# Wide and narrow products of an expert chunk: interleaved, or eight and then eight

## The chip, the cores and the metric

One core of a Trainium2 chip runs the whole program in one launch. The time is device microseconds of that core; the figure to compare is the median of the runs. An engine here is TensorE (PE, matrix products; PEld is its weight load), VectorE (DVE), ScalarE (ACT), GpSimd (POOL) or SyncE (SP, which only issues transfers).

## What is computed

Two transformer blocks over 256 tokens of width 1024. Only the last part of the second block matters here, a PEER layer. Its experts are 16,384 rows of two tables, and a token uses 128 of them (8 heads of 16), with softmax weights g:

```python
u = jnp.take(u_tab, experts, axis=0)
v = jnp.take(v_tab, experts, axis=0)
act = jax.nn.gelu(jnp.einsum('td,thkd->thk', xb, u)) * g
return jnp.einsum('thk,thkd->td', act, v)
```

The kernel doesn't gather. It multiplies all tokens by the whole table u, in 128 chunks of 128 experts, takes the gelu, multiplies by a dense matrix of weights that is zero for experts not picked, and multiplies the result by the whole table v.

## The kernel before

**Products in three terms.** Every operand is held as the sum of two fp32r parts, a leading part and a rest. For a slab of weights (128 x 1024, a ring of three buffers `ring`, filled by SyncE), ScalarE copies the leading part into `wsplit[:, n, 0]` (`lead_scalar`, line 267), and VectorE or GpSimd subtracts it from the slab to give the low part `wsplit[:, n, 1]` (`rest_of`, line 273). `wsplit` has three buffers as well. GpSimd does the subtractions of chunks 0 to 117, VectorE those of the last ten. `hsplit` holds both parts of the tokens.

**One chunk.** `split_project_wide` makes a chunk: for each of eight 128-row pieces c, a 512-column product of the leading weights with both parts of the tokens (line 2735), and a 256-column product of the low weights with the tokens' leading part (line 2739), added to the upper 256 columns of the same PSUM bank. Both halves of the bank are added later. Chunks use banks 3, 4 and 5 in turn, and a chunk waits until the one three before it has been joined. The function first waits for the low part (`slab_split`), which comes after the leading one.

**ring_used.** Each slab raises this semaphore once, by its first product. `lead_scalar` for slab s waits until slab s - 2 has raised it: then slab s - 3, the last user of its `wsplit` buffer, is finished. So the lead copy of chunk c + 3 waits for the signal of chunk c + 1. SyncE refills a ring buffer when its subtraction is done.

**Early chunks, 0 to 53.** TensorE does chunk after chunk. ScalarE's order for chunk c: copy the upper half of the bank (the low copy, line 2763), lead copy of chunk c + 3, gelu of chunk c - 1 (line 2770). VectorE works through the top-16 picks of the layer and in between joins the halves of chunk after chunk (`joined_vector`, line 2782). At the end TensorE transposes the picks and VectorE sets up operands (lines 2870 to 2874).

**Spread batches, chunks 54 to 117.** There are 64 batches b, with chunk c = 54 + b. TensorE: chunk c, then eight small products (line 2923) of one-hot operands for four tokens, which wait for both operands of batch b (`hot` of 2b + 2), then the next chunk. ScalarE in its written order, with the waits that matter:

```python
low_scalar(act, c)                     # line 2950, waits for chunk c
lead_scalar(act, *chunk_of(c + 3))     # line 267, waits for ring_used
...                                    # weights of batch b, line 2964
gelu_scalar(act, c)                    # lines 2943, 2944
```

VectorE for batch b: first operand of batch b + 1 (`found_vector`, line 2979), join of chunk c (line 2955), second operand of batch b + 1 (`hot_vector`, line 2985), then a multiply over all chunks so far (line 3008, waits for line 2964), then the weighted product of chunk c (`late_vector`, line 2992, waits for the gelu). In the last two batches a subtraction (line 273) stands between line 2979 and line 2955.

**Last chunks, 118 to 127**: chunk after chunk again, with subtractions on VectorE. After them TensorE opens the outputs and the value slabs begin (line 424), twelve 512-column products each.

Of the kernel before, what the change touches and what calls it, by code (L numbers as in the profile page):

```python
# [31 lines left out]
P = 128  # L32
D = 1024
KC = D // P
T = 256
# [4 lines left out]
RING = 3  # L40
# [86 lines left out]
def build(nc, weights, small, tables, masks, w3, decay, subkeys, gain_row, x, out):  # L127
# [3 lines left out]
    def S(stage, what):  # L131

        name = f"{stage}_{what}"
        if name not in sems:
            sems[name] = ctx.enter_context(nc.semaphore(name))
        return sems[name]

    def sb(name, shape, dt=F32):
        return ctx.enter_context(nc.sbuf_tensor(name, shape, dt))

    ring = sb("ring", [P, RING, D])
    wsplit = sb("wsplit", [P, RING, 2, D], F32R)
    hsplit = sb("hsplit", [P, 2, KC, T], F32R)
# [18 lines left out]
    ps = ctx.enter_context(nc.psum_tensor("ps", [P, 8, 512], F32))  # L162
# [95 lines left out]
    def split_index(stream, k):  # L258
        return SPLIT[stream] + k
# [16 lines left out]
    def slab_split(pe, stream, k, i, per=6):  # L276

        which, before = RESTS[stream]
        pe.wait_ge(S("split", which), i * per + (before + k + 1))
        return split_index(stream, k) % RING  # L280
# [2448 lines left out]

    def split_project_wide(pe, bank, stream, k, i=0, per=6):  # L2730

        n = slab_split(pe, stream, k, i, per)
        both = ps[:, bank, :].rearrange("p (b t) -> p b t", b=2)
        for c in range(KC):
            mm = pe.matmul(both, wsplit[:, n, 0, c * P:(c + 1) * P], hsplit[:, :, c, :],  # L2735
                           start=(c == 0), stop=(c == KC - 1), skip_group_check=True)
            if c == 0:
                mm.then_inc(ring_used, 1)
            mm = pe.matmul(ps[:, bank, T:2 * T], wsplit[:, n, 1, c * P:(c + 1) * P], hsplit[:, 0, c, :],  # L2739
                           start=False, stop=(c == KC - 1), skip_group_check=True)  # L2740
        return mm

    def early_tensor(pe, st, stream):
        pe.wait_ge(S("final", "x_rows"), 2)
        for k in range(3):
            wide_tensor(pe, st, stream, k)
        with pe.Fori(0, EARLY // 6 - 1) as i:
            for k in range(3, 9):
                pe.wait_ge(S(st, "joined"), i * 6 + (k - 2))
                split_project_wide(pe, hidden_bank(k), stream, 16 + k, i).then_inc(S(st, "hidden"), 1)  # L2750
        for c in range(EARLY - 3, EARLY):
            wide_tensor(pe, st, stream, c)

    def wide_tensor(pe, st, stream, c):
        if c >= 3:
            pe.wait_ge(S(st, "joined"), c - 2)
        s, k = chunk_of(c)
        split_project_wide(pe, hidden_bank(c), s, k).then_inc(S(st, "hidden"), 1)
# [714 lines left out]
```

## Time and profile before

| | |
|---|---|
| Median of 3 runs | 1884.05 us (1883.6 to 1887.24) |
| Profiled execution, its time | 1885.56 us |
| Its span, first to last instruction | 1883.7 us |
| TensorE, VectorE, ScalarE, GpSimd busy | 98%, 74%, 55%, 18% |
| Granted TensorE clock, mean | 0.998 |
| Expert chunks, first to last product | 1128.7 to 1528.3 us of the span |

Times in rows are us from the start of the span, unless marked ns. "x16" is a number of instructions. What stands in brackets behind an instruction is how long its engine was idle before it, and what ended that. The products overlap each other: the distance from start to start is what one costs, and not its length.

### The profile page before, as it was taken

How to read it: one execution, taken by the hardware profiler on the slowest of the kernel's cores; microseconds unless marked ns; L12 is line 12 of the kernel's file. 1: busy time of each engine (PE TensorE's matmuls, PEld its weight loads, DVE VectorE, ACT ScalarE, POOL GpSimd, SP SyncE). 2: the span in 40 equal slices, each digit the busy share in tenths (PEclk: the TensorE clock that was granted, in tenths of full speed). 3: DMA queues.
4: the chain of work that ended last, by engine and by line, in shares of the span. 5: the costliest groups of instructions: out<-in, count | busy, mean ns of one | idle time of the engine just before them, and what ended most of it. 6: DMA issues, size and time to landing. Idle time of an engine off the chain costs nothing.

```text
span 1883.7 us, 32317 instructions
## 1 busy us (share of the span) xinstructions
PE 1853.5 (98%) x11238; PEld 1602.5 (85%) x11238; DVE 1401.9 (74%) x2658; ACT 1042.4 (55%) x1817; POOL 331.4 (18%) x145
## 2 busy tenths in 40 slices
PE   9999999999999999999999999999999999999998
PEld 7877887788888889999999998888888888888887
DVE  7785566667655568898997678977999976666666
ACT  6666455656644466667555555565665543333333
POOL 0000000000000000000000168886777400000000
PEclk9999999999999999999999999999999999999999
DMA  6624655443455544443445445554444455555554
GB/s 217 224 78 148 216 174 178 145 146 124 146 189 189 187 147 157 147 135 124 136 145 175 155 143 181 186 189 152 162 157 161 155 187 192 196 191 191 196 193 156
DMA packets 86157, 314.11 MB, mean 167 GB/s; under 512 B 9568, under 2 KB 9696, under 8 KB 85856
## 3 DMA queue, kind: packets, MB, share of 16 engines
q1 hardware_dynamic: 86048, 312.65, 49.2%
q8 instruction: 69, 1.13, 0.2%
q14 instruction: 40, 0.33, 0.1%
HBM read 311.56 MB, written 1.05 MB: 166 GB/s over the span
## 4 chain that ended last, share of the span: by engine, by line
PE 83%; DVE 13%; ACT 2%; issue 2%; DMA 0%; SPq 0%; DVEq 0%; ACTq 0%
PE ps L424 24%; PE ps L409 14%; PE ps L2735 11%; PE ps L290 6%; PE ps L1967 6%; PE ps L2739 6%; PE ps L2537 3%; DVE wsplit L273 3%; PE ps L819 2%; PE ps L2036 2%; PE ps L2923 1%; DVE sq L2979 1%; PE ps L440 1%; ACT wsplit L267 1%; DVE work L2300 1%
## 5 line engine op out<-in xcount | busy, mean ns | idle before, releaser
L267 ACT ACTIVATE wsplit<-ring 128x1024 fp32r<-128x1024 f32 x572 | 603.8, 1059 | 450.5 <-PE ps L424 265.4
L273 DVE TENSOR_TENSOR wsplit<-ring,wsplit 128x1024 fp32r<-128x1024 f32 x440 | 541.5, 1235 | 304.8 <-ACT wsplit L267 303.8
L424 PE MATMUL ps<-wsplit,gsplit 128*128 128x512 f32 x1992 | 456.5, 390 | 0.0
L424 PEld LDWEIGHTS ps<-wsplit,gsplit 128*128 128x128 f32 x1992 | 373.2, 188 | 81.3 <-issue 4.0
L273 POOL TENSOR_TENSOR wsplit<-ring,wsplit 128x1024 fp32r<-128x1024 f32 x132 | 317.2, 2404 | 664.5 <-ACT wsplit L267 664.2
L2735 PE MATMUL ps<-hsplit,wsplit 128*128 128x512 f32 x1024 | 368.6, 403 | 0.0
L409 PE MATMUL ps<-wsplit,hsplit 128*128 128x512 f32 x1248 | 298.1, 394 | 4.5 <-DVE wsplit L273 3.4
L2739 PE MATMUL ps<-hsplit,wsplit 128*128 128x256 f32 x1024 | 286.4, 280 | 0.0
L409 PEld LDWEIGHTS ps<-wsplit,hsplit 128*128 128x128 f32 x1248 | 231.6, 188 | 55.5 <-DVE wsplit L273 7.3
L290 PE MATMUL ps<-hsplit,wsplit 128*128 128x256 f32 x1956 | 253.6, 287 | 2.6 <-DVE hsplit L340 1.5
L290 PEld LDWEIGHTS ps<-hsplit,wsplit 128*128 128x128 f32 x1956 | 239.8, 191 | 10.4 <-issue 4.5
L2735 PEld LDWEIGHTS ps<-hsplit,wsplit 128*128 128x128 f32 x1024 | 193.1, 189 | 43.9 <-issue 0.4
L2739 PEld LDWEIGHTS ps<-hsplit,wsplit 128*128 128x128 f32 x1024 | 193.9, 189 | 0.0
L1967 PE MATMUL ps<-hsplit,wsplit 128*128 128x256 f32 x936 | 128.2, 288 | 0.0
L1967 PEld LDWEIGHTS ps<-hsplit,wsplit 128*128 128x128 f32 x936 | 115.9, 190 | 0.0
L792 POOL TENSOR_TENSOR sq<-sq 128x512 f32<-128x512 f32 x9 | 14.0, 1558 | 495.3 <-ACT sq L773 494.5
L2979 DVE TENSOR_TENSOR sq<-ps,picks 128x1024 f16<-128x1024 f32 x64 | 77.6, 1212 | 0.0
L2985 DVE TENSOR_TENSOR sq<-sq,ps 128x1024 f16<-128x1024 f16 x64 | 77.3, 1208 | 0.0
L2537 PE MATMUL ps<-hsplit,wsplit 128*128 128x256 f32 x576 | 71.1, 284 | 1.3 <-DVE hsplit L2518 0.9
L2537 PEld LDWEIGHTS ps<-hsplit,wsplit 128*128 128x128 f32 x576 | 69.6, 192 | 2.3 <-DVE wsplit L273 1.5
L2950 ACT ACTIVATE eyeiota<-ps 128x256 f32<-128x256 f32 x74 | 28.4, 384 | 67.1 <-PE ps L2739 66.2
L2078 ACT ACTIVATE work<-work 128x256 f32<-128x256 f32 x128 | 48.6, 430 | 23.0 <-DVE work L2220 17.0
(346 smaller groups left out, 1900.3 us busy)
## 6 DMA issues: line engine op xcount, KB each, us to landing
ring<-in_weights SPq DMA_DIRECT2D x572, 512.0 KB, 3.3
work<-in_weights SPq DMA_DIRECT2D x8, 512.0 KB, 5.8
work<-in_tables SPq DMA_DIRECT2D x1, 1995.0 KB, 9.8
work<-in_decay SPq DMA_DIRECT2D x2, 512.0 KB, 5.0
work<-in_subkeys SPq DMA_DIRECT2D x2, 512.0 KB, 4.4
out_x<-work SPq DMA_DIRECT2D x4, 256.0 KB, 2.4
gains_x<-in_x SPq DMA_DIRECT2D x3, 256.0 KB, 6.1
work<-in_small SPq DMA_DIRECT2D x1, 591.0 KB, 8.1
```

The lines of the kernel that those rows point to most:

```text
L267: act.activation(wsplit[:, n % RING, 0, :], slab(s), ACT.Copy).then_inc(S("split", "lead"), 1)
L273: eng.tensor_tensor(wsplit[:, n % RING, 1, :], slab(s), wsplit[:, n % RING, 0, :], ALU.subtract).then_inc(S("split", RESTS[stream][0]), 1)
L290: mm = pe.matmul(dst, wsplit[:, n, a, c * P:(c + 1) * P], h[:, b, :], start=(c == 0 and t == 0), stop=(c == KC - 1 and t == 2))
L409: mm = pe.matmul(ps[:, bank + tt, :], hsplit[:, b, c, tt * P:(tt + 1) * P], wsplit[:, n, a, cc * 512:(cc + 1) * 512], start=(c == 0 and t ...
L424: mm = pe.matmul(YR[:, tt, half * 512:(half + 1) * 512], gsplit[:, slot, b, tt * P:(tt + 1) * P], wsplit[:, n, a, half * 512:(half + 1) * ...
L1967: mm = pe.matmul(dst, wsplit[:, n, a, c * P:(c + 1) * P], hsplit[:, b, c, :], start=(c == 0 and t == 0), stop=(c == KC - 1 and t == 2))
L2078: ins = act.activation(strided(mixed, (l % 2 * 2 + x_) * T, [[2 * size, n], [size, 2], [1, size]]), strided(qakb, x_ * 2 * T, [[2 * size, ...
L2537: mm = pe.matmul(branch(m), wsplit[:, n, a, c * P:(c + 1) * P], hsplit[:, b, c, :], start=(c == 0 and t == 0), stop=(c == KC - 1 and t == 2))
L2735: mm = pe.matmul(both, wsplit[:, n, 0, c * P:(c + 1) * P], hsplit[:, :, c, :], start=(c == 0), stop=(c == KC - 1), skip_group_check=True)
L2739: mm = pe.matmul(ps[:, bank, T:2 * T], wsplit[:, n, 1, c * P:(c + 1) * P], hsplit[:, 0, c, :], start=False, stop=(c == KC - 1), skip_group ...
L2979: v.tensor_tensor(hots[:, b % 2, 0:2, :, :], strided(ps, 2 * 512, [[0, 2], [0, 4], [1, P]]), picks[:, 0:2, batch(b)].unsqueeze(3).to_broad ...
L2985: v.tensor_tensor(hots[:, b % 2, 2:4, :, :], hots[:, b % 2, 0:1, :, :].to_broadcast([P, 2, 4, P]), strided(ps, 2 * 512 + P + 4 * b, [[T if ...
```

## The change

The chunk waits for the leading weights alone, does its eight 512-column products, waits for the low part, and does its eight 256-column ones. The signal `ring_used` moves from the first wide product to the first narrow one. The products, their operands and the number of semaphore signals stay. All 128 chunks use this function; the value slabs and all other stages don't.

```diff
-        n = slab_split(pe, stream, k, i, per)
+        pe.wait_ge(S("split", "lead"), i * per + (split_index(stream, k) + 1))
+        n = split_index(stream, k) % RING
         both = ps[:, bank, :].rearrange("p (b t) -> p b t", b=2)
         for c in range(KC):
-            mm = pe.matmul(both, wsplit[:, n, 0, c * P:(c + 1) * P], hsplit[:, :, c, :],
-                           start=(c == 0), stop=(c == KC - 1), skip_group_check=True)
+            pe.matmul(both, wsplit[:, n, 0, c * P:(c + 1) * P], hsplit[:, :, c, :],
+                      start=(c == 0), stop=(c == KC - 1), skip_group_check=True)
+        slab_split(pe, stream, k, i, per)
+        for c in range(KC):
+            mm = pe.matmul(ps[:, bank, T:2 * T], wsplit[:, n, 1, c * P:(c + 1) * P], hsplit[:, 0, c, :],
+                           start=False, stop=(c == KC - 1), skip_group_check=True)
             if c == 0:
                 mm.then_inc(ring_used, 1)
-            mm = pe.matmul(ps[:, bank, T:2 * T], wsplit[:, n, 1, c * P:(c + 1) * P], hsplit[:, 0, c, :],
-                           start=False, stop=(c == KC - 1), skip_group_check=True)
         return mm
```

## Rows read from the trace of the kernel before

**Rows 1.** The page, busy time, share and instructions of each engine.

```profile
PE 1853.5 (98%) x11238; PEld 1602.5 (85%) x11238; DVE 1401.9 (74%) x2658; ACT 1042.4 (55%) x1817; POOL 331.4 (18%) x145
```

**Rows 2.** The page, chain that ended last, shares by line.

```profile
PE ps L424 24%; PE ps L409 14%; PE ps L2735 11%; PE ps L290 6%; PE ps L1967 6%; PE ps L2739 6%; PE ps L2537 3%; DVE wsplit L273 3%; PE ps L819 2%; PE ps L2036 2%; PE ps L2923 1%; DVE sq L2979 1%; PE ps L440 1%; ACT wsplit L267 1%; DVE work L2300 1%
```

**Rows 3.** Stretches that begin and end with a chunk: busy us, clock, DMA.

```profile
1128.73:1281.46 152.73, 152.73 (x868) 132.53 (x866) 123.59 (x328) 93.27 (x164) 128.81 (x55) 1.00 0.55 183
1287.76:1292.54 4.78, 4.78 (x28) 4.06 (x25) 3.59 (x6) 1.93 (x5) 2.39 (x1) 0.66 0.24 93
1292.54:1470.38 177.84, 177.84 (x1300) 152.91 (x1298) 173.43 (x270) 107.55 (x271) 128.85 (x54) 1.00 0.48 159
1470.38:1498.89 28.51, 27.41 (x197) 22.75 (x194) 28.51 (x42) 16.06 (x41) 15.17 (x7) 1.00 0.42 142
```

**Rows 4.** Timeline of an early chunk, which starts at 1137.30.

```profile
1137.30 0.40 PE L2735 MATMUL ps<-hsplit,wsplit 128*128 128x512 f32 x1
...
1137.53 0.28 PE L2739 MATMUL ps<-hsplit,wsplit 128*128 128x256 f32 x1
...
1139.05 2.41 POOL L273 TENSOR_TENSOR wsplit<-ring,wsplit 128x1024 fp32r<-128x1024 f32 x1 [0.55 <-ACT wsplit L267]
...
1140.32 0.39 ACT L2763 ACTIVATE work<-ps 128x256 f32<-128x256 f32 x1 [1.04 <-PE ps L2739]
```

**Rows 5.** Chain that ended last: stretches of 256-column, then 512-column products.

```profile
1101.38 2.88 PE ps L290 x24
...
1528.65 342.97 PE ps L424 x1512
```

**Rows 6.** Timeline of the early spread batches, all engines; chunk start 1302.42.

```profile
1302.42 0.47 PE L2735 MATMUL ps<-hsplit,wsplit 128*128 128x512 f32 x1
...
1302.99 1.06 ACT L267 ACTIVATE wsplit<-ring 128x1024 fp32r<-128x1024 f32 x1 [0.42 <-PE ps L2735]
...
1303.96 0.39 ACT L2964 ACTIVATE work<-ps 128x280 f32<-128x280 f32 x1
...
1304.45 0.40 DVE L3008 SCALAR_TENSOR_TENSOR work<-ps,work 128x232 f32<-128x232 f32 x1 [0.23 <-ACT work L2964]
...
1304.76 0.17 DVE L2992 TENSOR_TENSOR work<-ps,work 128x20 f32<-128x20 f32 x1
...
1304.85 1.22 DVE L2979 TENSOR_TENSOR sq<-ps,picks 128x1024 f16<-128x1024 f32 x1
...
1305.28 0.62 PE L2923 MATMUL ps<-sq 128*128 128x128 f16 x8
...
1305.72 0.47 PE L2735 MATMUL ps<-hsplit,wsplit 128*128 128x512 f32 x1
1305.98 0.42 DVE L2955 TENSOR_TENSOR ps<-ps,eyeiota 128x256 f32<-128x256 f32 x1
...
1306.31 1.21 DVE L2985 TENSOR_TENSOR sq<-sq,ps 128x1024 f16<-128x1024 f16 x1
```

**Rows 7.** Timeline of the late spread batches, VectorE, ScalarE and TensorE.

```profile
1482.08 0.21 ACT L2964 ACTIVATE work<-ps 128x64 f32<-128x64 f32 x1
...
1483.39 0.61 DVE L3008 SCALAR_TENSOR_TENSOR work<-ps,work 128x448 f32<-128x448 f32 x1
...
1483.93 0.39 DVE L2992 TENSOR_TENSOR work<-ps,work 128x236 f32<-128x236 f32 x1
...
1484.24 1.21 DVE L2979 TENSOR_TENSOR sq<-ps,picks 128x1024 f16<-128x1024 f32 x1
...
1497.19 1.21 DVE L2985 TENSOR_TENSOR sq<-sq,ps 128x1024 f16<-128x1024 f16 x1
...
1498.46 0.62 PE L2923 MATMUL ps<-sq 128*128 128x128 f16 x8 [1.10 <-DVE sq L2985]
```

**Rows 8.** Chain that ended last, in chunk 55: start, us, what.

```profile
1288.75 0.43 PE ps L2735
1289.18 0.21 PE ps L2739
```

**Rows 9.** Timeline of TensorE at the first spread batch.

```profile
1287.24 0.66 PE L2923 MATMUL ps<-sq 128*128 128x128 f16 x7 [2.18 <-DVE sq L2985]
```

## The prediction

> **What bounds the kernel.** The page first: TensorE is busy 98% of the span, VectorE 74%, ScalarE 55% [rows 1], and the chain that ended last is TensorE products for 83% of it; the two lines of this function, L2735 and L2739, hold 17% [rows 2]. So what lengthens or shortens TensorE's own stream counts in full, and what another engine delays counts as soon as TensorE waits for it. The table by stretches splits the expert stage, which lies from 1128.7 to 1528.7 us: 54 early chunks (1128.73 to 1281.46), where TensorE never rests and VectorE is busy 124 of 153 us; and 64 spread batches, where between two chunks TensorE also does eight small products (L2923) with operands that VectorE builds. Of 178 us in the middle of these VectorE is busy 173, and of the last 28.5 us all [rows 3]. VectorE is the engine without room there, and I read the change against it.
>
> **The products.** The 54 early chunks take 1281.46 - 1128.73 = 152.7 us, 2.83 each [rows 3], so one of the eight pairs (512 then 256 columns) takes 0.353: about 0.235 from the start of the wide to that of the narrow [rows 4] and 0.12 from there on. Like after like is known from other stages: 1512 products of 512 columns took 342.97 us, 0.227 each, and 24 of 256 columns 2.88 us, 0.120 each, every one with its own weight load [rows 5]. The new chunk is then 8 x 0.227 + 8 x 0.120 = 2.78, 0.05 less. If the wide ones, whose right operand comes here as two runs of 256, keep the 0.236 that they show now, it is 8 x 0.236 + 8 x 0.120 = 2.85, 0.02 more. I take 0.05 less, by the 1512 rows. The 64 chunks where TensorE alone sets the pace (54 early, ten last) bring -3.2 us, between -3.4 and +1.3.
>
> The Trainium skill (TensorE: Matmul & The Clock Gate, Back-to-back issue gap) gives columns/2.4 GHz + 2.5 ns for a product by itself, which makes an estimate of 8 x 216 + 8 x 109 ns = 2.60 us for a chunk in either order. The rows show 2.83, and by the rule this part would be worth nothing instead of -3.2 us.
>
> **The later wait for the low part.** The chunk now starts on the leading weights alone and wants the rest eight products later. No chunk start waits for a rest in the trace, so this removes nothing; all it gives is room.
>
> **The later signal.** ring_used was raised by the first wide product and is now raised by the first low one, behind eight wide ones. ScalarE's lead copy of chunk c+3 (L267) waits for chunk c+1's signal, and already today it is what that copy waits for: chunk start 1302.42, copy 1302.99, 0.42 us of idle put down to L2735 [rows 6]. So the copy comes 0.57 after the chunk start, 0.10 after the product's end (0.47 long). In the new order the first low product starts at 0.08 (the first product of a batch's chunk is 0.47 long [rows 6], others 0.40 [rows 4]) + 8 x 0.227 = 1.89, lasts 0.28 and signals 0.10 later: 2.27. The copy is 1.70 us later than now.
>
> What stands behind it on ScalarE, in its fixed order: the copy of the batch's weights (L2964), the gelu, and the next chunk's low copy (L2950). VectorE waits for L2964 to do its long multiply (L3008), then L2992, then the compare (L2979), the join (L2955, which also waits for the low copy, done about 0.8 us earlier) and the second operand (L2985) that TensorE needs for the small products of the batch after next. Start to start from rows 6, for an early batch:
>
> chunk start c+1 to lead copy 2.27; to L2964 0.97; to L3008 0.49; to L2992 0.31; to L2979 0.09; to L2955 1.13; to L2985 0.33; to TensorE's L2923 1.27 [rows 7]; to the start of chunk c+3 0.44. Sum 7.30 us from chunk c+1 to c+3.
>
> Today the same path takes 7.30 - 1.70 = 5.60, less than two periods of 3.29 (6.58), so it is hidden with 0.98 us to spare. With 7.30 it is the longest loop: 3.65 us a batch, and TensorE waits for L2985 in every batch. Late in the stage L3008 and L2992 are longer and L2964 is shorter: L2964 to L3008 at least 0.31 (0.21 long, and 0.10 as for the early ones: 0.49 - 0.39), to L2992 0.54, to L2979 0.31 [rows 7]; the others stay. Sum 7.57, 3.79 a batch. The mean is 3.72.
>
> The 63 periods from chunk 55 to chunk 118 take 1498.89 - 1287.76 = 211.1 us now [rows 3]. Afterwards: 63 x 3.72 = 234.4; + 1.1 for the subtraction that VectorE takes over between L2979 and L2955 for the last two batches (one VectorE step from L2979 to what follows, and paid now too); + 1.5 at the beginning, because chunk 55 runs at half clock (a wide product 0.43 [rows 8]), which makes its eight wide ones 8 x 0.43 = 3.4 instead of 1.8. Together 237.0: +25.9 us.
>
> **At the edges.** In the early stage the low copy of a chunk now stands behind the previous lead copy (released 1.82 + 0.28 + 0.10 = 2.20 after the chunk start) and a gelu of 0.3 to 0.4: 2.20 + 0.97 + 0.35 = 3.52 instead of 1140.32 - 1137.30 = 3.02 [rows 4] after the chunk start. TensorE reuses that bank two chunks later, 5.7 us, so nothing waits, except at the end, where low copy 53, join 53 and the operand set-up lead to the first small products after 2.18 us of TensorE idle [rows 9]: +0.5. The rest of a slab is still ready: lead at 2.20, 1.06 long, GpSimd 2.41 long [rows 4], with its start 5.8 in all, wanted at 2 x 2.83 + 1.82 = 7.5; the refill of the ring shifts with both its ends. At the other edge the third value slab's lead copy stands behind a later gelu, some +0.4, an estimate with 0 and 1.5 as ends.
>
> Sum: 25.9 - 3.2 + 0.5 + 0.4 = +23.6. The profiled execution took 1885.56 us (span 1883.7, 1.9 around it): 1909.2. That execution is 1.5 over the median of the timed runs (1884.05), so against the median 1907.7; I say **1908**.
>
> **Bounds of the loop.** It has nine links, each read to 0.02, and the release depends on the 0.227: with 0.236 it is 0.07 later, 0.035 a batch, +2. Should an engine's link be 0.1 shorter when it is woken by a semaphore and not by its queue, or longer, a batch changes 0.05 and the whole 3. Two such either way, and the ends of the other terms: 1901 to 1915 for this case.
>
> **Rivals.** (a) The late lead copy is hidden and only the denser stream counts. For it: ScalarE has idle time in front of the lead copy already [rows 6], and rests have 1.7 us of room. Against: the order on both engines is written out, and the path above is over 6.58 by 0.7. It decides at the point where L2985 still starts within 1.56 us of its chunk's start (2.83 - 1.27). Then 128 chunks x 0.05 = -6.1: 1878 to 1882 against the median, faster. Chance 0.08.
> (b) Neither gain nor loss: the products cost what they did (0.353 a pair) and the path is hidden: 1884. Chance 0.04.
> (c) The early stage stalls as well, because VectorE, which works through the picks between joins, gets each low copy 0.5 later and falls behind; against it: VectorE has 153 - 124 = 29 us without work there [rows 3]. If a quarter of the joins pass their 0.5 on, +7: 1915. Chance 0.07.
> (d) TensorE's clock. It is below full in one stretch, chunk 55 (0.66 on average [rows 3], products of 0.43 and 0.21, half clock), right after the 2.18 us idle; the pair takes 0.64 there [rows 8, 9]. Idle of about 0.45 us in every batch could bring that back. The idle of 1.1 us at 1498.46 [rows 7] was followed by no fall: the stretches on both sides of it are granted in full [rows 3]. If half of the 62 batches ran at 8 x 0.64 + 0.9 = 6.0 us instead of 3.72, it is +71: near 1980. Chance 0.03. The Trainium skill (TensorE: Matmul & The Clock Gate, A second HAM failure mode: psum-queue depth-cycling) says that frequent short idles between groups of products can make the clock swing; this trace, with its 1.1 us gap at full clock, speaks against it.
> (e) My forecast, the loop through the lead copy and VectorE's operands: 0.78.
>
> **Range and chances.** 0.78 within 1901 to 1915 mostly; taking in half of (c) and room for links that I read too coarsely, **1898 to 1917** holds 8 in 10. What can be told from no change here is about 0.2%, 3.8 us (the three runs span 3.6). Slower by more: (c), (d), (e) = 0.88; faster by more: most of (a), 0.07; within: 0.05.
>
> **What would show it.** Right: the mean of 63 periods between chunks 55 and 118 is 3.6 to 3.85 and not 3.29 to 3.45; L2923 idles some 0.4 to 0.5 us for L2985 in about 60 batches; L267 starts 2.2 to 2.3 after its chunk start; L3008 waits for L2964 in nearly every batch; VectorE's busy share of 1292 to 1470 falls from 98% to under 90%. Early chunks take 2.78. Wrong: periods still at 3.29 (then an order of work that I take as fixed isn't), early periods over 2.85 (the wide ones cost more one after another), TensorE waits for GpSimd's rests in the middle of chunks, or the granted clock falls a second time.

## The result, and the profile after

The changed kernel takes 1909.96 us, median of 4 runs (1909.03 to 1910.71), against 1885.64 for the kernel before, timed again beside it: ratio 1.0129, 95% interval 1.0115 to 1.0143. It is slower by 24 us. Forecast were 1908 and 1898 to 1917.

The two executions that were profiled differ by 25.0 us of span. Of the page of the changed kernel (span, busy time, chain by engine and by line), against [rows 1, 2]:

```profile
span 1908.7 us, 32365 instructions
...
PE 1861.0 (97%) x11238; PEld 1608.8 (84%) x11238; DVE 1401.5 (73%) x2658; ACT 1034.7 (54%) x1817; POOL 331.2 (17%) x145
...
PE 78%; DVE 16%; ACT 3%; issue 3%; DMA 0%; DVEq 0%; SPq 0%; ACTq 0%
```

The number of instructions is the same, and TensorE's share of the chain is 78% where it was 83%: what was added is time in which TensorE waits. (TensorE's busy time is 7.5 us longer too; most of that is waiting as well, as shown below.) Lines are three higher than before from here on: the wide products are L2736, the narrow ones L2740, the small ones L2926, VectorE's L2982, L2958, L2988, L3011 and L2995 are [rows 6]'s L2979, L2955, L2985, L3008 and L2992.

The table by stretches shows where. Its columns are start and end, length, busy us of TensorE, of its weight loads, of VectorE, ScalarE and GpSimd (with the number of instructions), granted clock, DMA share and GB/s. The first stretch is the early chunks 0 to 52, the second the 63 periods from chunk 55 to chunk 118, where a period is the time from one chunk's start to the next one's:

```profile
1129.28:1277.42 148.14, 148.14 (x852) 130.37 (x851) 120.87 (x327) 89.70 (x160) 124.67 (x53) 1.00 0.55 182
1286.89:1523.74 236.85, 219.10 (x1517) 185.59 (x1514) 208.08 (x317) 119.53 (x315) 146.31 (x61) 0.99 0.42 139
```

The spread batches grew from 211.1 us [rows 3] to 236.85, with TensorE busy 219. The early chunks went the other way, 2.795 us each instead of 2.828. By the starts of single chunks in both traces the 25.0 us are: 25.7 in those 63 periods, -1.8 in the early chunks, +0.4 between chunk 54 and 55, -0.3 in the last ten chunks, +0.4 from there to the end, and 0.6 before the stage, where nothing was changed: in the traces of this study chunk 0 starts anywhere from 1128.2 to 1129.7.

The waits of the same 63 periods (who waited for whom: us in total, times, longest):

```profile
ACT wsplit L267 <- PE ps L2740: 118.6, 63, 5.1
...
PEld ps L2926 <- DVE sq L2988: 28.8, 57, 1.4
DVE work L3011 <- ACT work L2967: 28.0, 50, 2.6
PE ps L2926 <- DVE sq L2988: 17.1, 34, 1.2
```

ScalarE's lead copy waits in all 63 for the narrow product that now raises the signal; VectorE's multiply waits behind that copy 50 times; and TensorE's small products wait for VectorE's operand. Two batches from the timeline show the loop closed (line numbers L2967 and L2995 are the weights copy and the weighted product):

```profile
1328.36 2.09 PE L2736 MATMUL ps<-hsplit,wsplit 128*128 128x512 f32 x8
...
1330.07 1.21 DVE L2988 TENSOR_TENSOR sq<-sq,ps 128x1024 f16<-128x1024 f16 x1
1330.29 1.11 PE L2740 MATMUL ps<-hsplit,wsplit 128*128 128x256 f32 x8
...
1330.66 1.06 ACT L267 ACTIVATE wsplit<-ring 128x1024 fp32r<-128x1024 f32 x1 [1.97 <-PE ps L2740]
...
1331.34 0.62 PE L2926 MATMUL ps<-sq 128*128 128x128 f16 x8
...
1331.63 0.36 ACT L2967 ACTIVATE work<-ps 128x252 f32<-128x252 f32 x1
1331.77 2.09 PE L2736 MATMUL ps<-hsplit,wsplit 128*128 128x512 f32 x8
...
1332.09 0.43 DVE L3011 SCALAR_TENSOR_TENSOR work<-ps,work 128x260 f32<-128x260 f32 x1 [0.81 <-ACT work L2967]
1332.44 0.20 DVE L2995 TENSOR_TENSOR work<-ps,work 128x48 f32<-128x48 f32 x1
1332.55 1.21 DVE L2982 TENSOR_TENSOR sq<-ps,picks 128x1024 f16<-128x1024 f32 x1
1333.68 0.42 DVE L2958 TENSOR_TENSOR ps<-ps,eyeiota 128x256 f32<-128x256 f32 x1
1334.01 1.21 DVE L2988 TENSOR_TENSOR sq<-sq,ps 128x1024 f16<-128x1024 f16 x1
...
1335.28 0.62 PE L2926 MATMUL ps<-sq 128*128 128x128 f16 x8 [0.47 <-DVE sq L2988]
...
1335.71 2.09 PE L2736 MATMUL ps<-hsplit,wsplit 128*128 128x512 f32 x8
```

From chunk start 1328.36: lead copy 2.30, then 0.97, 0.46, 0.35, 0.11, 1.13, 0.33, 1.27, 0.43: 7.35 us to the start of the chunk after next, 1335.71. The two periods between share this sum unevenly, 3.41 and 3.94.

TensorE is held in both of them, though the profile shows idle only in the long one. In every batch from chunk 56 to chunk 117 the small products start 1.26 to 1.27 us after L2988 does, so the operand always sets their start. In the short batch above that is 2.98 us after the chunk's start; with the loop open it is 2.88 (below). A wait that short doesn't show as idle: the narrow products before it are drawn to 1331.40, beyond the start of the small ones at 1331.34. This is most of the difference between the idle of the products in the table of waits (17.1 us, of which the 1.1 in the last batch were there before the change, [rows 7]) and the time that was lost (25.7 us).

### The profile page after: what moved, and what is told of

Read it like the earlier page. It is cut to its first block, busy times and chain, and to the rows that moved or that the text cites. A ratio compares the mean times of both kernels' runs of the same rounds, so it can differ in the third digit from the quotient of the medians.

```text
span 1908.7 us, 32365 instructions
## 1 busy us (share of the span) xinstructions
PE 1861.0 (97%) x11238; PEld 1608.8 (84%) x11238; DVE 1401.5 (73%) x2658; ACT 1034.7 (54%) x1817; POOL 331.2 (17%) x145
## 3 DMA queue, kind: packets, MB, share of 16 engines
q8 instruction: 69, 1.13, 0.2%
## 4 chain that ended last, share of the span: by engine, by line
PE 78%; DVE 16%; ACT 3%; issue 3%; DMA 0%; DVEq 0%; SPq 0%; ACTq 0%
PE ps L424 24%; PE ps L409 13%; PE ps L2736 9%; PE ps L290 6%; PE ps L1967 6%; PE ps L2740 3%; DVE wsplit L273 3%; PE ps L2537 3%; DVE sq L2982 2%; DVE sq L2988 2%; PE ps L819 2%; PE ps L2036 2%; ACT wsplit L267 1%; PE ps L2926 1%; DVE work L3011 1%
## 5 line engine op out<-in xcount | busy, mean ns | idle before, releaser
L2736 PE MATMUL ps<-hsplit,wsplit 128*128 128x512 f32 x1024 | 262.9, 399 | 0.0
L290 PE MATMUL ps<-hsplit,wsplit 128*128 128x256 f32 x1956 | 253.6, 287 | 2.6 <-DVE hsplit L340 1.4
L290 PEld LDWEIGHTS ps<-hsplit,wsplit 128*128 128x128 f32 x1956 | 239.8, 191 | 10.4 <-issue 4.5
L2736 PEld LDWEIGHTS ps<-hsplit,wsplit 128*128 128x128 f32 x1024 | 183.9, 189 | 33.4 <-issue 0.4
L2740 PEld LDWEIGHTS ps<-hsplit,wsplit 128*128 128x128 f32 x1024 | 140.5, 191 | 10.4
L2740 PE MATMUL ps<-hsplit,wsplit 128*128 128x256 f32 x1024 | 143.2, 283 | 0.0
L1967 PE MATMUL ps<-hsplit,wsplit 128*128 128x256 f32 x936 | 128.2, 288 | 0.0
L1967 PEld LDWEIGHTS ps<-hsplit,wsplit 128*128 128x128 f32 x936 | 115.9, 190 | 0.0
L2982 DVE TENSOR_TENSOR sq<-ps,picks 128x1024 f16<-128x1024 f32 x64 | 77.7, 1214 | 0.0
L2988 DVE TENSOR_TENSOR sq<-sq,ps 128x1024 f16<-128x1024 f16 x64 | 77.4, 1209 | 0.0
L2537 PE MATMUL ps<-hsplit,wsplit 128*128 128x256 f32 x576 | 71.1, 284 | 1.3 <-DVE hsplit L2518 0.9
L2537 PEld LDWEIGHTS ps<-hsplit,wsplit 128*128 128x128 f32 x576 | 69.6, 192 | 2.3 <-DVE wsplit L273 1.6
L2926 PE MATMUL ps<-sq 128*128 128x128 f16 x512 | 39.7, 220 | 20.4 <-DVE sq L2988 19.8
```

The source lines that it names most:

```text
L290: mm = pe.matmul(dst, wsplit[:, n, a, c * P:(c + 1) * P], h[:, b, :], start=(c == 0 and t == 0), stop=(c == KC - 1 and t == 2))
L1967: mm = pe.matmul(dst, wsplit[:, n, a, c * P:(c + 1) * P], hsplit[:, b, c, :], start=(c == 0 and t == 0), stop=(c == KC - 1 and t == 2))
L2537: mm = pe.matmul(branch(m), wsplit[:, n, a, c * P:(c + 1) * P], hsplit[:, b, c, :], start=(c == 0 and t == 0), stop=(c == KC - 1 and t == 2))
L2926: mm = pe.matmul(ps[:, 6 + b % 2, k * P:(k + 1) * P], hots[:, b % 2, 1, k, :], hots[:, b % 2, 2 + part, k, :], start=(part == 0), stop=(pa ...
L2982: v.tensor_tensor(hots[:, b % 2, 0:2, :, :], strided(ps, 2 * 512, [[0, 2], [0, 4], [1, P]]), picks[:, 0:2, batch(b)].unsqueeze(3).to_broad ...
L2988: v.tensor_tensor(hots[:, b % 2, 2:4, :, :], hots[:, b % 2, 0:1, :, :].to_broadcast([P, 2, 4, P]), strided(ps, 2 * 512 + P + 4 * b, [[T if ...
```

## The experiments

All times are medians, and each ratio is to runs of the kernel before on the same chip (1885.13 us, 1885.98 and 1886.15 in the three sets).

**Where the signal is raised.** The order of the change stays; only `ring_used` moves.

```diff
         for c in range(KC):
-            pe.matmul(both, ...)
+            mm = pe.matmul(both, ...)
+            if c == 0:                      # signal_wide3: c == 3, signal_wide6: c == 6
+                mm.then_inc(ring_used, 1)
...
-            if c == 0:
-                mm.then_inc(ring_used, 1)
```

> The changed kernel (eight wide products, then eight narrow ones, wait for the low part in the middle), but ring_used is raised by the first wide product again. Theory L (the whole loss is the loop that the late signal closes: ring_used, ScalarE's lead copy, the weights copy behind it, VectorE's multiply, compare and second operand, TensorE's small products): the lead copy starts 0.57 us after its chunk's start, the loop is 5.60 to 5.87 us over two batches and hidden again. What stays is the order: 64 chunks at 2.79 instead of 2.83 (-2.2), some 48 batches at 3.31 instead of 3.29 (+1.0): 1884.4, between 1882 and 1886. Rival O (the order itself costs: the run of wide or of narrow products slows other engines or the reading of operands): it stays near 1908 to 1910.

> The changed kernel, but ring_used is raised by the fourth wide product: 0.08 + 0.70 + 0.40 + 0.10 = 1.27 us after the chunk's start. Theory L is a threshold: the loop is 6.30 us early (3.15 a batch, under the 3.31 of TensorE's own work) and 6.57 late (3.29, under VectorE's 3.44), so it is still hidden: the time of the version with the first wide product within 1 us, 1883 to 1886. Rival P (each bit of delay costs in proportion, 24 us for 1.70): 0.70 later costs 10 us, 1894 to 1896.

> The changed kernel, but ring_used is raised by the seventh wide product: 0.08 + 1.38 + 0.40 + 0.10 = 1.96 us after the chunk's start, 0.31 before the changed kernel's. Theory L: loop 6.99 early and 7.26 late, 3.50 to 3.63 a batch, 63 x 3.565 + 2.3 = 226.9, +15.8 in the spread stage, -1.9 early, +0.9 at the edges: 1900 to 1901. Rival P (in proportion to the delay, 1.39 of 1.70 of 24 us): 1905. Rival O: 1910.

With the first wide product: 1884.54 us, ratio 0.9996 (0.9987 to 1.0005). With the fourth: 1883.84, 0.9994 (0.9985 to 1.0003). With the seventh: 1899.79, 1.0076 (1.0062 to 1.009). Chunks 55 to 118 of the three kernels, by the table of stretches:

```profile
1285.92:1496.31 210.39, 209.26 (x1517) 184.39 (x1514) 205.62 (x317) 125.18 (x315) 146.14 (x61) 1.00 0.47 156
```

```profile
1286.68:1499.33 212.65, 211.52 (x1516) 185.47 (x1513) 205.67 (x317) 124.53 (x315) 145.93 (x61) 0.99 0.48 155
```

```profile
1286.10:1511.30 225.20, 214.97 (x1517) 184.34 (x1514) 207.09 (x317) 119.41 (x315) 146.00 (x61) 1.00 0.44 146
```

Median against median, 0.7 us later costs nothing, 1.4 us later 15 and 1.7 us later 24: a threshold and then a slope, as a hidden loop gives, and not a cost in proportion. All three medians lie within 1 us of what the loop gave. (Of the 2.3 us between the first two stretches 1.5 are the clock: chunk 55 takes 4.80 us in the second execution, with 3.4 us at half clock, and 3.31 in the first. The rest lies mostly behind chunk 105, where VectorE sets the pace, and is not explained.) The order by itself, rival O, costs nothing.

**The signal late, in the old order.** The kernel before, with the signal on the sixth wide product:

```diff
-            if c == 0:
+            if c == 5:
                 mm.then_inc(ring_used, 1)
             mm = pe.matmul(ps[:, bank, T:2 * T], wsplit[:, n, 1, ...], hsplit[:, 0, c, :], ...)
```

> The kernel before with its alternating order, in which only the signal moves: ring_used is raised by the sixth wide product of a chunk and not by the first. It comes 0.08 + 5 x 0.353 + 0.40 + 0.10 = 2.35 us after the chunk's start, about as in the changed kernel (2.27). Theory L: loop 7.38 us early and 7.65 late, 3.69 to 3.82 a batch, 63 x 3.755 + 2.6 = 239.2 instead of 211.1, +0.9 at the edges, and no gain from the order: +29, 1914 to 1915. Rival O: the order is the old one, so the time of before, 1885.

Measured: 1922.62 us, 1.0196 (1.0182 to 1.021). Rival O is out once more, but it is 8 us over what the loop gives. The spread batches are not to blame: they take 236.59 us (239.2 expected, of which 1.5 were for a half clock that this execution doesn't show there). The excess lies where I had expected none, in the early chunks 0 to 52:

```profile
1129.69:1287.89 158.20, 157.39 (x852) 129.16 (x850) 122.61 (x327) 90.09 (x161) 125.21 (x53) 1.00 0.52 173
1297.49:1534.08 236.59, 215.71 (x1517) 179.10 (x1514) 207.78 (x317) 119.51 (x315) 146.17 (x61) 1.00 0.43 139
...
PEld ps L2735 <- POOL wsplit L273: 10.0, 38, 0.4
```

158.2 instead of 149.9 us, and the waits of the early stage name GpSimd's subtraction: TensorE stands at the start of the chunk for the low part.

**The wait for the low part at the start.** The changed kernel, with `n = slab_split(...)` back at the head of the function, in place of the wait for the leading part, and no wait between the wide and the narrow products. The wide products are L2735 here and the narrow ones L2738.

> The changed kernel, but the chunk waits for the low part at its start as before, and only the order of the products and the place of the signal are changed. Theory L: no wait for a rest is on any path, so 1908 to 1911, the changed kernel's time. Rival S (TensorE waits in the middle of chunks for low parts): the time moves by more than 2 us.

Measured: 1919.66 us, 1.0183 (1.0168 to 1.0198), 10 us over the changed kernel. My expectation was wrong, and rival S was right that the place of this wait matters, though the changed kernel itself never waits there. Timeline of the early chunks of this kernel:

```profile
1202.24 2.08 PE L2735 MATMUL ps<-hsplit,wsplit 128*128 128x512 f32 x8
...
1204.53 1.06 ACT L267 ACTIVATE wsplit<-ring 128x1024 fp32r<-128x1024 f32 x1 [1.23 <-PE ps L2738]
1205.26 1.68 PEld L2735 LDWEIGHTS ps<-hsplit,wsplit 128*128 128x128 f32 x8 [0.20 <-POOL wsplit L273]
1205.26 2.11 PE L2735 MATMUL ps<-hsplit,wsplit 128*128 128x512 f32 x8
1205.67 2.41 POOL L273 TENSOR_TENSOR wsplit<-ring,wsplit 128x1024 fp32r<-128x1024 f32 x1 [0.46 <-ACT wsplit L267]
...
1208.16 2.08 PE L2735 MATMUL ps<-hsplit,wsplit 128*128 128x512 f32 x8
```

Chunk start 1202.24, lead copy 2.29 later, subtraction 1.14 after that and 2.41 long: 5.84 us. The chunk that needs this low part starts 0.08 later, at 1208.16, so two chunks take 5.92, where they take 2 x 2.795 = 5.59 in the changed kernel. So there is a second loop, through GpSimd, that the late signal closes in the early stage. The change's other half, the wait in the middle of the chunk, gives it 1.8 us more (eight wide products) and hides it.

**The lead copy out of the way.** In the spread batches only ScalarE's order is changed; signal and products are those of the change.

```diff
             low_scalar(act, c)
-            lead_scalar(act, *chunk_of(c + 3))
             act.wait_ge(S(st, "weights"), b + 1)
             act.activation(peer_w[:, c:NKEYS, batch(b)], ...)
+            lead_scalar(act, *chunk_of(c + 3))      # weights_then_lead
             gelu_scalar(act, c)
+            lead_scalar(act, *chunk_of(c + 3))      # lead_after_gelu, in place of the one above
```

> The changed kernel, signal on the first narrow product, but on ScalarE the copy of the batch's weights stands ahead of the lead copy in the spread batches; the gelu stays behind it. Theory L: VectorE's multiply no longer waits behind the lead copy, but the weighted product waits for the gelu that does. Loop early: 2.27 + 0.97 + 0.25 + 0.27 + 0.09 + 1.13 + 0.33 + 1.27 + 0.44 = 7.02, late 7.26, so 3.51 to 3.63 a batch: 1900 to 1901. Rival S (TensorE waits for the slab itself, because its lead copy or its subtraction on GpSimd comes late): no change, 1908 to 1910.

> The changed kernel, signal on the first narrow product, but in the spread batches ScalarE does the lead copy last, behind the weights copy and the gelu. Nothing that VectorE needs stands behind the late signal any more. Theory L: the loop is open, batches take 3.31 (TensorE) to 3.44 (VectorE), the lead copy still starts about 2.3 us after the chunk's start: 1885, between 1883 and 1888. Rival S (the slab itself comes late): putting the lead copy behind two more instructions makes it no better or worse, 1908 or more.

Behind the weights copy: 1898.13 us, 1.0068 (1.0056 to 1.0081). Behind the gelu too: 1883.77, 0.9991 (0.9982 to 1.0). The signal is as late as in the changed kernel in both. Chunks 55 to 118 and who waits in them, for the first kernel:

```profile
1286.77:1511.19 224.42, 214.80 (x1517) 184.35 (x1514) 207.31 (x317) 121.61 (x315) 146.42 (x61) 1.00 0.45 147
...
DVE work L2995 <- ACT ps L2947: 16.0, 38, 1.3
```

and for the second:

```profile
1286.10:1496.41 210.31, 209.19 (x1517) 184.38 (x1514) 206.04 (x317) 125.91 (x315) 146.70 (x61) 1.00 0.48 156
...
ACT wsplit L267 <- PE ps L2740: 56.6, 59, 1.0
...
DVE ps L2958 <- ACT eyeiota L2953: 2.9, 14, 0.3
...
PEld ps L2926 <- DVE sq L2988: 1.7, 3, 1.3
```

and two lines of its timeline:

```profile
1329.17 2.09 PE L2736 MATMUL ps<-hsplit,wsplit 128*128 128x512 f32 x8
...
1332.05 0.62 PE L2926 MATMUL ps<-sq 128*128 128x128 f16 x8
```

In the first, VectorE now waits for the gelu (L2947), the next thing behind the lead copy; in the second the lead copy still waits for the narrow product 59 times. What stands behind it now is the next chunk's low copy (L2953), and VectorE's join (L2958) waits for that only 14 times, 2.9 us in all, which doesn't reach TensorE: its small products start 2.88 us after their chunk. That is the whole loss, and it shows the mechanism: not the late slab, but what stands in line behind its copy.

**Both loops apart.** The wait at the start and the lead copy behind the gelu together.

> The changed kernel with two edits together: the chunk waits for the low part at its start, and in the spread batches ScalarE does the lead copy last. Theory R (with the late signal there is a second loop, in the early chunks: release 2.20, lead copy 1.1, GpSimd's subtraction 2.4, over two chunks, which only the wait in the middle of the chunk keeps hidden): spread batches at 3.31 to 3.44 as in the run with the lead copy last (1883.8), early chunks at 2.97 to 2.98 as in the run with the wait at the start, 53 x 0.18 = 9.6 more: 1893 to 1894. Rival Q (the 10 us of the run with the wait at the start came with the slow spread batches, or belong to no stage in particular): under 1888, or a sum that doesn't lie in the early chunks.

Measured: 1895.02 us, 1.0038 (1.0025 to 1.0052), 1 us over what was expected.

```profile
1128.68:1286.52 157.84, 156.99 (x851) 132.97 (x850) 122.51 (x327) 90.06 (x161) 125.21 (x53) 1.00 0.53 173
1296.09:1506.41 210.32, 209.19 (x1516) 184.39 (x1514) 206.12 (x317) 125.94 (x315) 146.72 (x61) 1.00 0.48 156
```

The spread batches are whole again at 210.3, and the early chunks cost 157.84 - 148.14 = 9.7 us more, so rival Q is out: two loops, one in each stage.

**The order where it pays.** Early and last chunks in the new order, spread batches in the old, signal and wait as before the change:

```diff
+        if grouped:                          # not EARLY <= c < POOLED
+            for c in range(KC):
+                ...                          # eight wide, signal at c == 0
+            for c in range(KC):
+                ...                          # eight narrow
+            return mm
```

> The kernel before, signal on the first wide product and wait for the low part at the start, but the 54 early and ten last chunks do eight wide and then eight narrow products; the 64 spread batches alternate as before. By the stages measured: 54 x 0.033 + 10 x 0.033 = 2.1 less and no loss of 0.02 in the batches: 1883 against 1885, ratio 0.9989, at the edge of what can be told. If the order has no worth outside this bound, the interval holds 1.

Measured: 1884.04 us, 0.9986 (0.9977 to 0.9995). The early chunks are 148.14 us and the 63 periods 209.64 with no stretch at half clock in this execution. It is 0.14% under the kernel before: less than the 0.2% bound of the prediction, though its interval leaves out 1. It can't be told apart from the version with the lead copy behind the gelu (0.9991, 0.9982 to 1.0).

## Why the prediction was right

**The loop through the lead copy.** Forecast 7.30 us for two early batches and 7.57 for two late ones. Measured 7.35 above, and 7.57 for the two from chunk 114 to chunk 116; the mean period is 3.68 from chunk 57 to 85, 3.77 from 85 to 105 and 3.85 from 105 to 118. The 63 periods: 237.0 forecast, 236.85 measured; of this chunk 55 took 4.86 where the sum had 5.22, since the loop isn't closed there yet, and the other 62 periods 232.0 where it had 231.8. Each link but the first was a distance in the trace of before, and none changed by more than 0.04 when it became critical; the first, worked out as 2.27, is 2.30. The signs that I named came mostly true: lead copy 2.30 after its chunk's start; VectorE's share from chunk 56 on 180 of 204 us, 88%; no second stretch at half clock in the expert stage. These are the two stretches that follow chunk 55:

```profile
1291.75:1495.81 204.06, 189.57 (x1316) 160.47 (x1313) 179.57 (x276) 104.73 (x277) 131.54 (x56) 1.00 0.42 140
1495.81:1523.74 27.93, 24.68 (x177) 20.91 (x177) 26.28 (x39) 13.20 (x38) 14.31 (x6) 1.00 0.41 137
```

Two signs were off in form. TensorE is held for L2988 in all 62 batches from chunk 56 on, as forecast, but the 0.4 to 0.5 us of idle isn't spread evenly: the products show idle 34 times, mostly 0.4 to 0.6 us in every second batch and little or none between, and the weight loads 57 times, since the loop spans two batches and fixes only their sum. And the multiply waits in 50 batches, not in nearly all.

**The products.** The direction was right, but a third of the gain didn't come. Forecast 2.78 us a chunk, measured 2.795. The wide ones in a row don't start 0.227 but 0.227 to 0.236 apart. In the spread batches the new order is slower: 3.313 in the versions with the loop open against 3.293 before, which I had not foreseen. The term of -3.2 us was -1.8 early and -0.3 in the last ten, -2.1 together; with 0.02 more in each batch that TensorE paces, the order by itself comes to nothing that can be told (0.9996).

**The edges.** +0.5 and +0.4 forecast, +0.4 and +0.4 measured. The first is where I put it: TensorE is idle for 2.62 us before the first small products instead of 2.18. The second is so only by half. About 0.2 are at the third value slab, as forecast; the other 0.2 come before the value slabs, where the opening of the outputs (L2939) now waits for a join (0.17 us of idle put down to L2958), which I had not foreseen. The +1.5 for the half clock in chunk 55 fitted, since both profiled executions have it, but it isn't a property of the kernel: of the eleven traces three show it there. For two kernels that differ in this it is 1.5 us of noise (4.8 us against 3.31 for that chunk).

**The sum.** The terms of the forecast, 25.9 - 3.2 + 0.5 + 0.4 = 23.6, were 25.7 - 2.1 + 0.4 + 0.4 = 24.4 in the traces, and the medians differ by 24.3. The errors of the terms are 1.1 us at most, so the forecast doesn't rest on large errors that cancel. Most of the 2 us between 1908 and 1909.96 is the kernel before, which took 1884.05 in the runs that I started from and 1885.64 beside the changed one.

**The later wait.** "This removes nothing; all it gives is room" was right for what the change does to this kernel and hid how much hung on it: with the signal late, that room is worth 10 us. I had both numbers, 5.8 us for the slab and 2.83 (then 2.78) a chunk, and compared the 5.8 only with the new place of the wait. The same omission made two expectations wrong, by 8 us and by some 9 (1919.66 against 1908 to 1911). The forecast itself lost nothing by it, since in the changed kernel that loop stays hidden.

**The rivals.** (a) and (b), the path hidden, are ruled out by the waits. (c), joins late in the early stage, is not seen: TensorE is busy there without a break, 148.14 of 148.14 us. (d), the clock: with idle of mostly 0.4 to 0.6 us in every second batch it is granted in full from chunk 56 to 118 (the two stretches above). That is stronger than the single gap of 1.1 us that I had gone by. [rows 3] doesn't show the stretch behind that gap; in the same trace 1498.89 to 1528.65 is granted in full too. The Trainium skill's rule that frequent short idles between groups of products can make the clock swing (TensorE: Matmul & The Clock Gate, A second HAM failure mode: psum-queue depth-cycling) found no case here.

## What to carry to other kernels

Moving a semaphore's signal along a stream is a change of its own: look up who waits for it, and what stands behind that waiter in its engine's written order, since that is what gets late. Add the distances of the path once around, divide by the number of periods that it spans, and compare with the period. Below it the delay is free; above it each microsecond costs its share in every period (half a microsecond a batch here, where the loop spans two). Judge a wait by the distance from start to start, and not by idle alone: a third of the loss here shows as no idle. When a wait is relaxed in the same edit, work out the loop with the old wait as well; here the two halves of one edit had opposite effects, and the half that looked useless hid 10 us.

## What was not expected of the hardware

The distance between products depends on their neighbours by a few per cent. These are means of start-to-start distances in the traces. In the early chunks of the old order it is 0.237 us from a wide product to the narrow one and 0.117 from there to the next wide one, 0.354 a pair. In the new order the wide ones are between 0.227 and 0.236 apart, the last ones 0.227, the first narrow one starts 0.227 behind the last wide one, the second 0.113 behind the first, and the others are 0.120 apart. The sum over a chunk differs by 0.033 us between the two orders where chunks follow each other, and by 0.02 the other way where small products stand between them.

It is the old order that changes between the two stages. In the spread batches (chunks 57 to 105) its pairs take 0.350 and 0.343 by turns instead of 0.354. In the new order the distances from a chunk's second product to its last add up to the same in both stages, within 0.005. Why the old order gets faster there was not tried.
